# One loop over the input tiles for an expert pair's gate and up products

## The reference

```
def expert_block(args):
    tok, wt, ex = args
    xb = hf[tok]
    a = xb @ w_gate[ex]          # 1024 -> 512
    u = xb @ w_up[ex]            # 1024 -> 512
    y = (jax.nn.silu(a) * u) @ w_down[ex]    # 512 -> 1024
    return y * wt[:, None].astype(y.dtype)
```

## The kernel before

| unit | waits for the use of |
|---|---|
| gate b, half 0 | down b - 3 |
| gate b, half 1 | gate b - 1 |
| up b, half 0 | gate b - 1 |
| up b, half 1 | up b - 1 |
| down b, half 0 | up b |
| down b, half 1 | down b - 1 |

## Time and profile before

### The profile page before, as it was taken

The page is one execution under the profiler, slowest core; times in us unless marked ns, Lnnn a source line. Parts: engine busy times, 40 slices in busy tenths (PEclk is TensorE's granted clock), DMA queues, the critical chain, the costliest instruction groups (busy, mean ns, idle before and its releaser), DMA issues.

```text
span 3953.7 us, 39828 instructions
## 1 busy us (share of the span) xinstructions
PE 3454.4 (87%) x16724; PEld 2358.5 (60%) x16724; DVE 1106.1 (28%) x1759; ACT 1103.4 (28%) x1874; POOL 710.5 (18%) x344
## 2 busy tenths in 40 slices
PE   7987899979848988988879999988899986889896
PEld 5665578856537777756558877454686553333332
DVE  2633220132573333343331022246230121000001
ACT  3423342434432211212334342133321121111110
POOL 3121144422200000002114432000142121010001
PEclk9998899988878877879999999998999987999998
DMA  3321153321100000023112222210032235998996
GB/s 101 98 93 54 43 166 109 130 70 59 54 0 1 1 1 1 12 64 101 43 43 96 96 86 98 85 44 11 22 96 70 75 136 235 385 373 344 381 384 278
DMA packets 217760, 448.63 MB, mean 113 GB/s; under 512 B 14192, under 2 KB 191376, under 8 KB 204656
## 3 DMA queue, kind: packets, MB, share of 16 engines
q1 hardware_dynamic: 200832, 400.58, 27.8%
q10 hardware_dynamic: 6720, 25.17, 1.7%
q0 software_dynamic: 10032, 20.35, 1.5%
HBM read 502.67 MB, written 31.46 MB: 135 GB/s over the span
## 4 chain that ended last, share of the span: by engine, by line
PE 74%; DVE 11%; DMA 7%; ACT 4%; issue 3%; POOL 1%; SPq 0%; ACTq 0%; POOLq 0%; DVEq 0%
PE product_banks L526 12%; PE product_banks L528 12%; PE product_banks L527 12%; PE product_banks L505 7%; PE product_banks L1692 5%; DMA A<-in_w_up 3%; PE product_banks L1725 3%; DMA Wr<-expert_rows 3%; PE product_banks L561 2%; PE product_banks L2139 2%; PE stat_bank L599 2%; PE product_banks L2129 1%; PE product_banks L2131 1%; PE product_banks L965 1%; PE product_banks L1172 1%
## 5 line engine op out<-in xcount | busy, mean ns | idle before, releaser
L443 POOL TENSOR_TENSOR Wr_parts<-Wr,Wr_parts 128x1024 fp32r<-128x1024 f32 x266 | 639.4, 2405 | 1989.1 <-ACT Wr_parts L423 1989.1
L527 PE MATMUL product_banks<-A_parts,Wr_parts 128*128 128x512 f32 x2128 | 846.2, 398 | 0.0
L423 ACT ACTIVATE Wr_parts<-Wr 128x1024 fp32r<-128x1024 f32 x266 | 280.9, 1059 | 1043.9 <-PE product_banks L528 986.2
L526 PE MATMUL product_banks<-H_parts,Wr_parts 128*128 128x512 f32 x1168 | 478.7, 410 | 62.2 <-DVE A_parts L455 37.7
L527 PEld LDWEIGHTS product_banks<-A_parts,Wr_parts 128*128 128x128 f32 x2128 | 408.9, 192 | 99.7 <-issue 11.4
L528 PE MATMUL product_banks<-H_parts,Wr_parts 128*128 128x512 f32 x1168 | 468.2, 401 | 0.0
L526 PE MATMUL product_banks<-A_parts,Wr_parts 128*128 128x512 f32 x960 | 397.2, 414 | 46.9 <-POOL Wr_parts L443 31.3
L528 PE MATMUL product_banks<-A_parts,Wr_parts 128*128 128x512 f32 x960 | 378.8, 395 | 0.0
L1692 PE MATMUL product_banks<-A,Wr 128*64 128x512 f32 x1504 | 340.4, 600 | 19.4 <-DMA A<-in_w_up 17.1
L526 PEld LDWEIGHTS product_banks<-H_parts,Wr_parts 128*128 128x128 f32 x1168 | 224.1, 192 | 134.8 <-issue 42.1
L1692 PEld LDWEIGHTS product_banks<-A,Wr 128*64 128x64 f32 x1504 | 113.3, 139 | 241.7 <-issue 238.7
(11 more groups left out here) (392 smaller groups left out, 4147.6 us busy)
## 6 DMA issues: line engine op xcount, KB each, us to landing
A<-in_w_gate SPq DMA_DIRECT2D x32, 2048.0 KB
A<-in_w_up SPq DMA_DIRECT2D x32, 2048.0 KB
A<-in_w_down SPq DMA_DIRECT2D x32, 2048.0 KB
Wr<-in_m_w_up SPq DMA_DIRECT2D x32, 1024.0 KB, 5.3
Wr<-in_m_w_down SPq DMA_DIRECT2D x32, 1024.0 KB, 4.8
Wr<-in_w_in SPq DMA_DIRECT2D x32, 1024.0 KB, 5.7
Wr<-in_c_w_kv SPq DMA_DIRECT2D x16, 1024.0 KB, 5.1
expert_rows<-LB ACTq DMA_DIRECT2D x12, 1024.0 KB, 4.6
```

Source lines behind the costliest of these rows:

```text
L423: nc.scalar.activation(weight_parts(s)[0], loaded_part(s), ACT.Copy).then_inc(*mark("weights_high", s))
L443: nc.gpsimd.tensor_tensor(lo, loaded_part(s), hi, ALU.subtract).then_inc(*mark("weights_split", s))
L526: pe.matmul(bank[:, :], hi[:, k, :], x_hi, start=(kk == 0), stop=False)
L527: pe.matmul(bank[:, :], hi[:, k, :], x_lo, start=False, stop=False)
```

## The change

`pair_product_pe` goes away. `pair_up_pe` now first waits for the earlier pair's SiLU and its hidden product, and for all units of gate and up, and then runs one loop over the 8 input tiles with the gate and the up matmuls of each tile inside it. The mark `unit_used` of gate and the one of up are both put into the last tile's turn.

```
         def pair_up_pe(pe, b):
             pe.wait_ge(*at("pair_rows_ready", (b, 1)))
             if b:
                 pe.wait_ge(*at("silu_ready", b - 1))
+                pe.wait_ge(*at("hidden_ready", b - 1))
             else:
                 pe.wait_ge(*at("rows_known", 0))
-            pair_product_pe(pe, "gate", b)
-            if b:
-                pe.wait_ge(*at("hidden_ready", b - 1))
-            pair_product_pe(pe, "up", b)
+            for kind in ("gate", "up"):
+                for h in range(halves(b)):
+                    unit_ready(pe, (kind, b, h))
+            for k in range(8):
+                for n, kind in enumerate(("gate", "up")):
+                    for h in range(halves(b)):
+                        r = slice(CAP * h, CAP * h + CAP)
+                        mm = pe.matmul(BK[r, n, :],
+                                       XT[b % 2][:, k * P + CAP * h:k * P + CAP * h + CAP],
+                                       unit_rows((kind, b, h))[:, k, :], start=(k == 0),
+                                       stop=(k == 7))
+                    if k == 7:
+                        mm.then_inc(*mark("unit_used", (kind, b)))
```

More of the change, by code:

```diff
@@ L1684, in pair_turn_pe @@
             mm.then_inc(*mark("pair_rows_turned", b))
[L1686 to L1696, removed]
         def pair_up_pe(pe, b):
```

## The result

The changed kernel takes 4082.99 us (median of four runs, 4077.30 to 4088.17) against 3949.95 us for the kernel before (four runs). The ratio is 1.033, with a 95% interval of 1.0306 to 1.0354: 133 us more. The profiled execution took 4077.3 us. Its experts' stage begins 16 us earlier than in the trace of before (the first pair's products at 3299.78 against 3315.66). It is not counted as an effect of the change. The stage is therefore compared by itself, from the first pair's gate product to the end of the last down product.

What follows compares the result with a forecast made beforehand. Neither TensorE nor DMA has much to spare, so their release order bounds the stage. 7 x 15.0 = 105 plus 6.7 gives 111.7 us; 3955.45 + 111.7 - 5.4 = 4062 us, range 4025 to 4092 (81%).

Steps and rivals of the forecast that it cites:

- The period: Experts' stage, one extra pair and two main pairs: 91.5 us instead of 76.5, 15.0 more (bounds 12.3 to 19.1), seven times.
- The extra pair: Start of the next extra pair, after three indirect loads issued together: 0.5 us added, bounds 0 and 2.
- The flight from a standstill: Second main pair's 6.3 MB, issued once the DMA has finished earlier work: 18.2 us, landing at 65.5, bounds 64.5 and 67.5.
- the clock: TensorE's products after an idle of 7 to 9 us: 2.0 us longer, bounds 1.4 and 2.3.
- The first pairs: Stage start: 6.7 us at the first extra pair (5.2 wait, 1.5 clock), plus 15.0 for the main pairs after it.
- The last pairs: Stage end: the last extra pair has one half, so its neighbour's units are ahead by one: nothing.
- What I costed at nothing: In the pair products: bank changes in each step, the later SiLU, the earlier wait for the hidden product: 0 us.
- One stall only: Rival, 5%: second main pair's units land before TensorE is ready, a period grows by 5.4 us: 3994 us.
- Every pair stalls: Rival, 10%: extra pairs wait too, 35 us more, or each bank change costs 0.05 us, 17 more: 4079 to 4097.
- Nothing moves: Rival, 2%: the slots have more slack than read, with both changed waits inside it: 3950 us.
- Faster by an unbroken loop that keeps the clock up: Rival, 2%: merged burst waits for nothing, stage's 33 us of waits go, 3917 us; clock gives at most 11 us.

Runs made afterwards that it cites:

- The filler: Changed kernel plus eight 128-column matmuls into an unused bank ahead of each main pair's wait from b = 2 on: 4056.22 us, against 3954.43 for the kernel before.
- the late release: Kernel before, its loops and waits kept, only the mark releasing gate's slots moved to one input tile before the up product's end: 4016.63 us against 3954.43.

## Why the prediction was right, and where its sizes were off

The direction, the mechanism and its places were right. The median lies 21 us above the forecast of 4062 and inside its range of 4025 to 4092. In the stage of the trace the miss is 26 us (112 forecast, 138 measured). Point by point, in the stage:

- **The period** was forecast to grow by 15.0 us to 91.5; it grew by 17.4 to 94.0, inside the bounds that I gave. The terms, as means over the six full periods: the first main pair starts at 33.5, not 32.4; its product and the second pair's take 16.0 and 16.1 us, not 15.8; the second pair starts 18.5 us after the first one's end, not 17.3. The extra pair does not wait, where I had added 0.5. The flight from a standstill and the clock were mis-sized, each by less than the bounds.
- **The first pairs** were forecast at 6.7 + 15.0 = 21.7 us and cost 32.7 (127.8 us from the first pair's start to the first period's, against 95.2). For one group of pairs this is the largest miss, 11 us. In the timeline of PE:

```profile
3326.23 16.36 PE L1700 MATMUL product_banks<-A,Wr 128*64 128x512 f32 x64 [9.42 <-DMA A<-in_w_up,wrow]
...
3366.16 16.87 PE L1700 MATMUL product_banks<-A,Wr 128*64 128x512 f32 x64 [13.73 <-DMA A<-in_w_up]
```

  The first extra pair waited 9.4 us, since its indirect load took 10.4 us, not the median of 7.6, and 2.4 us of clock came on top. The main pair behind it waited 13.7 us. I took this group for one like the others, but its extra pair is the one that fetches real weights: between 3345 and 3362 us the queue of the indirect loads moved 2.1 MB, and over the six full periods 0.02 MB. Its down unit shares the DMA engines with the next pair's units. That the sharing makes up the difference is argued from the sizes, and not tried.
- **The last pairs** were forecast at nothing and cost 1.2 us.
- **What I costed at nothing** stayed there: 64 records with the bank changing in each step take 13.90 us, the SiLU's late start is not seen in any wait, and the hidden product's wait neither.
- **The rivals.** One stall only: refuted, the second main pair waits 8.1 us. Every pair stalls: refuted, the extra pairs inside the periods start without a wait. Nothing moves: refuted by 133 us. Faster by an unbroken loop that keeps the clock up: refuted. The loop is unbroken, yet the clock fell from 0.98 to 0.89, because the waits did not vanish but moved ahead of the loop and grew. The filler shows that they, not the products, took the clock. The Trainium skill ("TensorE: Matmul & The Clock Gate", table "Why this matters for your kernels") recommends for few rows to run all K tiles before the next DMA wait. This trace does not agree, for here the wait ahead of the loop grew from 2.0 to 9.2 us by it.

The shakiest point of my picture was not in the forecast but came out in the late release: I thought it small by itself, at 5 us, and it costs 62.

## What to carry to other kernels

In a ring of buffers a product does two things besides computing: it covers the flight of the next buffers, and its end releases its own. Merging two loops that share an input moves the first wait to the last operand's landing and the first release to the common end, and where transfers fill most of the time, as here, both are paid, while the shared loop gains nothing. If a loop must be merged, cut its buffers along the loop and wait and release by these pieces; and compare it with the separate loops on the same pieces, which were as fast or faster here. And look at what stands last in a load queue: half a megabyte of rows for each pair, issued one stage earlier, was worth 31 us here. When a second edit is laid on a first, take its price from a kernel that has the other edit already: 25 us over before looked like a price of 62 more than halved, and was one of 56.

## What the runs showed of the hardware beyond that

The length of an idle does not alone decide whether TensorE's clock falls. The 3.36 us wait of the earlier trace rows was followed by a product of 8.46 us (granted clock 0.83); in the same trace a wait of 3.40 us was followed by one at full clock:

```profile
3444.66 7.09 PE L1692 MATMUL product_banks<-A,Wr 128*64 128x512 f32 x32 [3.40 <-DMA A<-in_w_up]
```

In the kernel with the filler, 3.2 us of waiting left the pair behind it at 13.95 us, and 2.6 us of waiting in another period was followed by one of 15.65 us. The late release shows the price: waits of 2.4 and 4.3 us were followed by products 1.7 and 2.8 us longer, and one of 1.8 us by none. An indirect load whose indices fetch nothing still takes some time to signal its landing, 7.6 us in the middle for the up loads of before, though in the six full periods that queue moved 0.02 MB in all. It must be counted like a transfer where someone waits for it.
